# Hierarchical MoE step: expert rows weighted as they leave PSUM, and accumulated by DMA into the outputs

## What is computed

```python
def hierarchical_moe(h, ...):                     # h = rmsnorm(x1), t = its 320 rows
    g_prob = softmax(t @ w_router_group + b);  g_p, g_idx = top_k(g_prob, 1)
    e_prob = softmax(logits of the 8 experts of that group);  e_p, e_idx = top_k(e_prob, 2)
    e_p = e_p / sum(e_p);      combine = one_hot(e_idx) * e_p * g_p, by group
    for g in range(N_GROUPS):                     # dense in the reference
        hg = silu(t @ w_gate[e]) * (t @ w_up[e])
        out = out + (hg * combine[e]) @ w_down[e]
return x1 + out
```

## Time and profile before

| | us |
|---|---|
| median of three executions | 906.62 |
| the profiled execution, its own time | 908.45 |
| its span on the core | 907.0 |

### The profile page before, as it was taken

The page is one execution under the profiler, slowest core; times in us unless marked ns, Lnnn a source line. Parts: engine busy times, 40 slices in busy tenths (PEclk is TensorE's granted clock), DMA queues, the critical chain, the costliest instruction groups (busy, mean ns, idle before and its releaser), DMA issues.

```text
span 907.0 us, 14392 instructions
## 1 busy us (share of the span) xinstructions
PE 763.5 (84%) x5476; PEld 605.1 (67%) x5476; DVE 401.9 (44%) x936; ACT 300.8 (33%) x552; POOL 144.4 (16%) x245
## 2 busy tenths in 40 slices
PE   2999999977799898999778898989399999787780
PEld 1788999965456588999666678988274555444440
DVE  3574334454345443657455545773753222111113
ACT  5434354533323343556222224443421111111110
POOL 5001000002134200011231310000302222222210
PEclk9999999987789989999998989999699999999996
DMA  5233433223568615273575551893849999999985
GB/s 177 95 139 132 142 139 134 94 78 132 151 190 243 207 41 186 94 250 132 191 247 158 169 183 54 333 352 142 327 167 418 417 418 418 420 419 419 417 335 184
DMA packets 38170, 202.84 MB, mean 224 GB/s; under 512 B 7490, under 2 KB 8018, under 8 KB 18898
## 3 DMA queue, kind: packets, MB, share of 16 engines
q1 hardware_dynamic: 24434, 160.29, 46.0%
q0 software_dynamic: 13664, 41.58, 14.4%
HBM read 184.24 MB, written 23.38 MB: 229 GB/s over the span
## 4 chain that ended last, share of the span: by engine, by line
PE 54%; DMA 17%; DVE 13%; ACT 8%; issue 6%; POOL 0%; POOLq 0%; SPq 0%; DVEq 0%; ACTq 0%
PE bank L1677 18%; DMA fm<-in_w_moe 9%; PE bank L1681 7%; PE bank L2020 6%; DVE rm L1089 3%; PE bank L1832 3%; DMA em<-in_w_moe 3%; ACT rm L773 3%; PE bank L2040 3%; PE bank L1667 3%; PE bank L1881 2%; PE bank L1916 2%; PE bank L2001 1%; DMA fm<-in_cache_lf 1%; PE bank L1821 1%
## 5 line engine op out<-in xcount | busy, mean ns | idle before, releaser
L1677 PE MATMUL bank<-rm 128*128 128x320 f32 x1344 | 211.4, 317 | 2.4 <-issue 1.6
L1677 PEld LDWEIGHTS bank<-rm 128*128 128x128 f32 x1344 | 202.7, 193 | 7.7 <-issue 6.1
L1089 DVE TENSOR_TENSOR rm<-fm,rm 128x2048 fp32r<-128x2048 f32 x48 | 110.1, 2293 | 83.5 <-ACT rm L773 83.0
L1681 PE MATMUL bank<-rm 128*128 128x256 f32 x960 | 126.5, 292 | 7.2 <-DVE rm L1089 3.6
L1681 PEld LDWEIGHTS bank<-rm 128*128 128x128 f32 x960 | 122.1, 199 | 8.4 <-DVE rm L1089 3.8
L773 ACT ACTIVATE rm<-fm 128x2048 fp32r<-128x2048 f32 x48 | 91.9, 1915 | 25.7 <-PE bank L1677 16.9
L2022 PE MATMUL bank<-fm,em 128*64 128x256 f32 x384 | 96.6, 397 | 0.0
L2020 PE MATMUL bank<-em 128*64 128x256 f32 x272 | 68.1, 395 | 9.6 <-DMA fm<-in_w_moe 4.8
L2020 PE MATMUL bank<-fm,em 128*64 128x256 f32 x240 | 60.3, 397 | 12.6 <-DMA fm<-in_w_moe 11.3
L2020 PEld LDWEIGHTS bank<-em 128*64 128x64 f32 x272 | 36.2, 141 | 36.8 <-issue 22.1
L1052 ACT ACTIVATE fm<-bank 64x256 f32<-64x256 f32 x32 | 12.0, 376 | 136.5 <-PE bank L2022 136.5
(11 more groups left out here) (388 smaller groups left out, 1032.8 us busy)
## 6 DMA issues: line engine op xcount, KB each, us to landing
fm<-in_w_moe SPq DMA_DIRECT2D x57, 1024.0 KB, 26.6
fm<-in_w_dense SPq DMA_DIRECT2D x48, 1024.0 KB, 4.9
em<-in_w_moe SPq DMA_DIRECT2D x39, 1024.0 KB, 26.1
fm<-in_state_C POOLq DMA_DIRECT2D x32, 257.0 KB, 4.2
out_C_sample<-fm POOLq DMA_DIRECT2D x32, 257.0 KB, 5.3
fm<-in_cache_kT POOLq DMA_DIRECT2D x16, 512.0 KB, 5.0
fm<-in_cache_v POOLq DMA_DIRECT2D x16, 512.0 KB, 4.5
fm<-y_rows SPq DMA_DIRECT2D x4, 512.0 KB, 5.1
```

The lines of the kernel that those rows point to most:

```text
L1089: s(TT(pair[c % 2][1], cube(raw[c % RAW1], KC), pair[c % 2][0], ALU.subtract), sem("split_done"))
L1677: ins = mm(bank[b][:, 0:NT], w[:, k, P * u:P * (u + 1)], a[:, k, :], start=first, stop=final)
L1681: ins = mm(bank[b][0:r, 0:CW], a[:, k, TILE0[u]:TILE0[u] + r], w[:, k, :], start=first, stop=final)
```

## The change

Outputs take the place of `y_rows`. SP, not POOL, stores x1 three times: to `y_prompt`, to `y_sample` and to `x1_dram`, ahead of weight load 14; both waits for `x1_stored` now ask for all three. `hot` is widened to `hot_rw` (row number, and weight), and the matmuls for the row numbers become twelve of 64 columns instead of six of 32; they move ahead of `start(0)`. `w_slot` is each place's weight, and `take_y` multiplies by it: ACT by `scale`, DVE by a `tensor_scalar`. The DVE steps for ranks, weights and `at_rank` move in between the copies of the sort.

The experts run in another order: `expert(v)` takes one of each group in turn. So v and v + 1 (v even) are of different groups and share no token. POOL no longer scatters after each expert, but after each second one, both halves of `y_area` (128 rows) at once, as two indirect DMAs that add to what is there: one on `y_prompt`, one on `y_sample`. `take_y(v)` for v >= 2 waits for both DMAs of the pair before: 32 times the number of earlier pairs. The end goes: no reload of x1, no read-back, no combining, no output stores outside `crowd`.

```diff
-        y_rows = nc.dram_tensor("y_rows", [6 * P, D], F32).ap()
+        y_rows = O["y_prompt"].rearrange("p t d -> (p t) d")
...
+        def expert(v):
+
+            return v % NG * EPG + v // NG
...
-                sp.dma_start(slot[n % NSLOT], A["w_moe"][3 * v + j]).then_inc(landed(v, j)[0], 16)
+                sp.dma_start(slot[n % NSLOT], A["w_moe"][3 * expert(v) + j]).then_inc(landed(v, j)[0], 16)
...
                 elif n == 14:
+                    sp.wait_ge(sem("x1_full"), 1)
+                    sp.dma_start(O["y_prompt"], x1[:, 0:2, :]).then_inc(sem("x1_stored"), 16)
+                    sp.dma_start(O["y_sample"], x1[0:NS, 2, :]).then_inc(sem("x1_stored"), 16)
+                    sp.dma_start(x1_dram, x1).then_inc(sem("x1_stored"), 16)
...
-            pool.wait_ge(sem("x1_full"), 1)
-            pool.dma_start(x1_dram, x1).then_inc(sem("x1_stored"), 16)
...
                     pool.wait_ge(sem("e_y_left"), v + 1)
                     pool.wait_ge(sem("e_y_right"), v + 1)
-                    pool.indirect_dma_start(y_rows, bass.IndirectOffsetOnAxis(ap=row_i[:, v:v + 1].bitcast(U32), axis=0),
-                                            yrow[v % NY], None, bounds_check=6 * P - 1, oob_is_err=False)\
-                        .then_inc(sem(f"e_y_stored{v % NY}"), 16)
+                    if v % 2 == 0:
+                        continue
+                    for rows, place, n in ((y_rows, row_i, TP), (O["y_sample"], row_s, NS)):
+                        idx = place[:, expert(v - 1):expert(v - 1) + 1].bitcast(U32)
+                        pool.indirect_dma_start(rows, bass.IndirectOffsetOnAxis(ap=idx, axis=0), y_area, None,
+                                                bounds_check=n - 1, oob_is_err=False, compute_op=ALU.add)\
+                            .then_inc(sem("e_y_stored0"), 16)
...
                 act.wait_ge(sem("e_used"), unit(v, 2) + 1)
+                if v == 0:
+                    act.wait_ge(sem("rows_ready"), 1)
                 if v >= NY:
-                    act.wait_ge(sem(f"e_y_stored{v % NY}"), 16 * (v // NY))
-                A_(yrow[v % NY][:, 0:D // 2], bank[4 + v % 2][0:CAP, :], ACT.Copy).then_inc(sem("e_y_left"), 1)
+                    act.wait_ge(sem("e_y_stored0"), 32 * (v // NY))
+                A_(yrow[v % NY][:, 0:D // 2], bank[4 + v % 2][0:CAP, :], ACT.Copy,
+                   scale=w_slot[0:CAP, expert(v):expert(v) + 1]).then_inc(sem("e_y_left"), 1)
...
                 dve.wait_ge(sem("e_used"), unit(v, 2) + 1)
                 if v >= NY:
-                    dve.wait_ge(sem(f"e_y_stored{v % NY}"), 16 * (v // NY))
-                CP(yrow[v % NY][:, D // 2:D], bank[4 + v % 2][CAP:2 * CAP, :]).then_inc(sem("e_y_right"), 1)
+                    dve.wait_ge(sem("e_y_stored0"), 32 * (v // NY))
+                TSC(yrow[v % NY][:, D // 2:D], bank[4 + v % 2][CAP:2 * CAP, :], w_slot[CAP:2 * CAP, expert(v):expert(v) + 1],
+                    None, ALU.mult).then_inc(sem("e_y_right"), 1)
...
-            dve.wait_ge(sem("xe_in"), 16 * 3)
-            s(CP(wts[NS:P, 2, :], wts[0:NS, 2, :]))
-            for t in range(3):
-                n = D if t < 2 else D // 2
-                dve.wait_ge(sem(f"rows_of_y{t}"), 32 if t < 2 else 64)
-                for k in range(2):
-                    s(STT(xe[:, t, 0:n], gat[2 * t + k][:, 0:n], wts[:, t, k:k + 1], xe[:, t, 0:n], ALU.mult, ALU.add),
-                      sem("y_done") if k else None)
...
-            start(0)
             pe.wait_ge(sem("onehot"), 3 + 6)
             for k in range(2):
                 for t in range(3):
                     i, r = 3 * k + t, ROWS[t]
-                    ins = mm(bank[6][0:CAP, 0:NE], at_rank[i][0:r, :], hot[k][0:r, t, :], start=(i == 0), stop=(i == 5))
+                    for half in range(2):
+                        ins = mm(bank[6][CAP * half:CAP * (half + 1), 0:2 * NE], at_rank[i][0:r, :], hot_rw[k][0:r, t, :],
+                                 start=(i == 0), stop=(i == 5), skip_group_check=True)
             ins.then_inc(sem("router_full"), 1)
+            start(0)
```

The DVE part of the sort, shortened:

```diff
+            for n in range(1, 2 * KC, 2):
+                k, half = n // 2, n % 2
+                dve.wait_ge(sem("sorted_full"), n + 1)
+                s(CP(xs[:, k, NT * half:NT * (half + 1)], bank[n % 4][:, 0:NT]), sem("sorted_free_v"))
+                if k < 2:
+                    ranks(k)
+                elif k == 2:
+                    combine()
+                elif k < 5:
+                    hot_rows(k - 3)
+                elif k < 7:
+                    at_ranks(k - 5)
```

More of the change, by code:

```diff
@@ L317, in hybrid_step @@
         offs = take(NE)
+        hot_rw = [cube(take(3 * 2 * NE), 3) for _ in range(2)]
         assert top[0] <= FW
+        w_slot, not_sample = (fm[:, base_masks + 1296 + NE * i:base_masks + 1296 + NE * (i + 1)] for i in range(2))
         squares, lgT = em[:, 12288 + 384:12288 + 384 + CW], em[:, 12288 + 640:13312]
@@ L498, in _ @@
                 load(n)
[L500 to L503, removed]
             def crowd():
+                sp.wait_ge(sem("blocks_stored"), 1)
+                sp.dma_start(xe[:, 0:2, :], x1_dram[:, 0:2, :]).then_inc(sem("xe_in"), 16)
+                for rows, w in SIDES:
+                    sp.dma_start(xe[rows, 2, 0:D // 2], x1_dram[0:NS, 2, w]).then_inc(sem("xe_in"), 16)
                 sp.wait_ge(sem("xe_in"), 16 * 3)
@@ L514, in crowd @@
                                 .then_inc(c_in, 16)
-            for u in range(NY):
-                sp.wait_ge(sem(f"e_y_stored{u}"), (NE - u + NY - 1) // NY * 16)
-            for t in range(2):
-                for k in range(2):
[L520 to L525, removed]
-            either(sp, crowd, sp.nop)
-            for t in range(3):
[L529 to L535, removed]
+                for t in range(3):
+                    sp.wait_ge(sem("y_done"), t + 1)
+                    if t < 2:
+                        sp.dma_start(O["y_prompt"][:, t, :], xe[:, t, :]).then_inc(sem("y_out"), 16)
+                    else:
+                        for rows, w in SIDES:
+                            sp.dma_start(O["y_sample"][:, w], xe[rows, t, 0:D // 2]).then_inc(sem("y_out"), 16)
+                sp.wait_ge(sem("y_out"), 16 * 4)
+            either(sp, crowd, sp.nop)
         @block.gpsimd
@@ L700, in run_experts @@
                 pool.wait_ge(sem("rows_ready"), 1)
+                pool.wait_ge(sem("x1_stored"), 16 * 3)
                 for v in range(NE):
@@ L1539, in _, with ranks @@
             s(v.tensor_reduce(most[:, 0:1], bank[4][:, 0:NE], AX_X, ALU.max))
[L1540 to L1549, removed]
+            def ranks(k):
                 s(TT(esel, hot[k], offs.unsqueeze(1).broadcast_to([P, 3, NE]), ALU.mult))
@@ L1552, in _, with combine @@
                 s(TT(scal[3 * k], place[:, :, k], scal[3 * k + 1], ALU.subtract))
[L1553 to L1560, removed]
+            def combine():
                 dve.wait_ge(sem("router_exps"), 1)
@@ L1567, in late_words, with hot_rows, at_ranks @@
                 s(TT(wts[:, :, 1], wts[:, :, 0], second, ALU.mult))
+            def hot_rows(k):
+                s(TT(hot_rw[k][:, :, 0:NE], hot[k], row_of.unsqueeze(2).broadcast_to([P, 3, NE]), ALU.mult))
+                s(TT(hot_rw[k][:, :, NE:2 * NE], hot[k], wts[:, :, k:k + 1].broadcast_to([P, 3, NE]), ALU.mult))
+            def at_ranks(k):
+                for t in range(3):
+                    s(TSC(at_rank[3 * k + t][0:ROWS[t], :], iota[0:ROWS[t], 0:CAP], scal[3 * k][0:ROWS[t], t:t + 1], None,
+                          ALU.is_equal), sem("onehot"))
+            dve.wait_ge(sem("x1_stored"), 16 * 3)
+            s(v.memset(xs[:, :, SLOTS:XC], 0.0))
+            for n in range(1, 2 * KC, 2):
[10 more added lines that the diff above has]
+                    at_ranks(k - 5)
+            dve.wait_ge(sem("sorted_free_a"), KC)
+            s(v.memset(small[0:1, 94:95], 0.0), sem("xs_ready"))
+            dve.wait_ge(sem("router_full"), 6)
+            s(TSC(not_sample, bank[6][:, 0:NE], float(TP - NO_ROW), float(NO_ROW), ALU.is_lt, ALU.mult))
+            for part, w, o in ((slice(0, CAP), slice(0, NE), slice(0, NE)),
+                               (slice(CAP, 2 * CAP), slice(EPG, NE), slice(0, NE - EPG))):
+                s(TSC(row_i[part, o], bank[6][part, w], float(NO_ROW), None, ALU.add))
+                s(STT(row_s[part, o], bank[6][part, w], float(NO_ROW - TP), not_sample[part, w], ALU.add, ALU.add))
+            s(CP(w_slot, bank[6][:, NE:2 * NE]), sem("rows_ready"))
+            def late_words():
                 crowd3 = crowd_i.rearrange("p (t k) -> p t k", t=3)
@@ L1612, in crowd @@
                 dve.wait_ge(sem("c_free"), NE * JB + 1 + 4)
[L1614 to L1623 removed]
+                s(CP(wts[NS:P, 2, :], wts[0:NS, 2, :]))
+                for t in range(3):
+                    n = D if t < 2 else D // 2
+                    for k in range(2):
```

(3 more changed lines are left out.)

32 lines of the change are left out of this document (16 added, 16 removed).

## The result

The changed kernel takes 938.5 us in the median (934.5 to 943.1) against 907.5 for the kernel before on the same chip: a ratio of 1.036, interval 1.031 to 1.041. It is slower, by 3.6%. The forecast was slower by 1.7%. The profiled execution of after took 935.45 us.

What follows compares the result with a forecast made beforehand. PE sets the pace first, the weight stream later, then a tail without weights. First pair at 690.6, twelve pairs of 16.2 us to 885.0, plus 32.9 and 5, make 922.9; less 0.4, rounded to 922 us, range 894 to 948.

Steps and rivals of the forecast that it cites:

- the chain behind the wait: From a pair's landing through take_y, htp copy, down matmuls and copy to POOL's next issue: 4.7 us.
- the tail: After the last copy, from the last pair's first issue to the kernel's end: 5 us, bounds 3.5 and 9.
- The wait itself: take_y of the next expert waits until both DMAs of the pair before land; a pair takes 16.2 us.
- Start of the experts: Row-number matmuls add 1.2 to 2 us, moved DVE steps save 1.1; first pair issued at 690.6, within 1 us.
- The store of x1: Moved to SP's queue ahead of load 14, landed at about 652 before DVE's wait at 660.31: cost 0.
- L: From a pair's first issue to its second DMA's landing, under the weight stream: 11.5 us, later 5 us.
- the formula: Landing time: 4.1 us lead, 0.31 us per packet for a load packet plus its own time, 0.5 to land.
- the third rival: Accumulates cost two turns or wait on memory, 958 us; or PE's clock is lower in gaps, 950 us; chance 0.10.
- slots that never hold the loads: Weight stream: 21 slots hold seven experts and six are left after pair 12, so slots don't hold the loads.
- The last three pairs: After the weights end: two pairs at PE's 11.2 us and a last one of 8.9, 32.9 us with the clock.
- The tail that goes: Landing, read-back, combining and stores after the last issue, 20.4 us before, shrink to 5: gain 15.4 us.

Runs made afterwards that it cites:

- e2: Changed kernel plus six useless matmuls on PE ahead of each second expert's downs, v = 3 to 29: 1.040 of the kernel before.
- e4: Changed kernel with plain writes instead of additions in the pair's DMAs: 1.019 of the kernel before, 922.6 us.
- e6: Changed kernel with a second y_area in place of one weight slot and the closing wait on SP: 0.988 of the kernel before, 895.5 us.
- e9: e6 without the addition, so that the DMAs overwrite: 0.982 of the kernel before, 890.9 us.
- e5: Changed kernel with the closing wait for the accumulating DMAs on SP instead of POOL: 1.030 of the kernel before, 936.5 us.
- e8: Changed kernel plus six useless matmuls on PE ahead of odd experts' downs only up to v = 25: 1.031 of the kernel before, 934.4 us.

## Why the prediction was right in sign and short in size

The step that failed is the chain behind the wait: it was put at 4.7 us and measured 6.2, since the gap that the wait makes lets PE's clock fall and the down matmuls take 2.8 to 3.7 us instead of 1.9 (e2 gives the 4.7 back). A second term, the tail, was put at 5 us and measured 9.6. The wait itself, its place and its landing were right.

The span was forecast at 922.9 and is 934.0. The 11.1 us are four terms: -7.0 at the start, +10.6 in twelve pairs, +2.9 in the last three, +4.6 after the last issue.

- **Start of the experts** (forecast 690.6, measured 683.65). The moved edits cost nothing, as forecast: from the issue of the x1 store to the first pair it took 54.0 us before and 53.7 after (630.00 to 683.65). The 7 us come from ahead of the change. PE ran for 44 us at its lower clock before 620 us, against 68 in before, and over the ten kernels profiled with the change the first pair's issue lay between 683.0 and 692.3, on the whole later the more such time there was (44 to 72 us). Why one execution has more of it than another isn't settled. It also means that the forecast, put on a start like before's, would have missed by 18 us, not 11: that the miss is no larger is luck.
- **The store of x1**: three stores, issued at 630.0 to 631.1, landed when DVE passed its wait at 654.19 with 0.17 us idle. Its cover held.
- **L** (forecast 11.5; measured 11.4 to 12.0 in eight of the ten long pairs, 12.4 and 13.0 in two, mean 11.85). The term that the case hung on was right. Its parts were 4.8 us of lead, not 4.1, and 0.33 us a data packet, as assumed. With the 4.8 the formula gives 12.2, so it is good to some 0.4 us and no better. The Trainium skill (DMA: Bandwidth & Descriptors, section "Anatomy of one DMA"), with about 2.0 us plus bytes at 436 GB/s, would have it near 5 by the prediction's estimate: the runs show 11.4 to 13.0 us beside a full load queue and 5.6 to 6.1 once the weights are in. For the landing that a wait sees, the rule was of use here only with the queue of the loads empty.
- **The chain** (forecast 4.7, measured 5.7 to 6.5, mean 6.2): the step that failed. Its down matmuls were priced at the 1.9 us of a stretch without gaps, though the forecast itself makes the gap of 4 to 5 us before each of them. The lower clock was named, in the third rival, as a possible load on PE's slack, with 17.5 us a pair; it belonged in the forecast's own chain. The rival's 950 puts 17.5 on all sixteen pairs, though the last three have no weights beside them: in the forecast's own sum it gives 690.6 + 12 x 17.5 + 32.9 + 5 = 938.5. Measured, 11.85 + 6.2 make the 18.0 us that ten of twelve pairs took, 1.8 over the forecast: 1.5 by the chain and 0.35 by L. `take_y` with its factor took 0.76, not 0.69; copy to issue 1.61, not 1.53.
- **Gaps in the weight stream.** The forecast had slots that never hold the loads. In two pairs SP waited for slots and the load queue was short all the same, and they got off with 12.3 us, 3.9 under the forecast each. So ten pairs at +1.8 and two at -3.9 make the +10.6; without the two gaps, which the forecast did not have, the miss would have been larger. PE never waited for weights, as forecast: no weight load stands among what released it. The weights ended at 885.5, also as forecast.
- **The last three pairs** (forecast 32.9, measured 35.8). The forecast took the last one at PE's pace, 8.9 us; it is the chain again and took 12.6: 6.1 us to the release, 6.5 with the slow downs. The two before took 11.56 by POOL's longer issues; with plain writes (e4) they took 11.18.
- **The tail** (forecast 5, measured 9.6): 5.6 to landing, then POOL's DRAIN. The view that would have shown it is the list of the closing instructions, in which before has its 5.2 us hidden.
- **The tail that goes** was worth what was said, seen without the wait: in e6 7.6 us follow the last issue instead of 20.4, and 12.8 are gained. 2.1 of them are lost again, as the last issue is at 888.73 instead of 886.62; without the added reads (e9) it is at 882.54. That leaves the 10.7 us between the spans 907.0 and 896.3. These are single executions, whose first pairs were issued 8.2 us apart (691.29 and 683.05); the medians are 8.7 us apart (904.2 and 895.5).

## What to carry to other kernels

When a transfer takes over work, ask who waits for its landing, and price that landing beside the traffic that will run there: here it was 18 packets an engine, each behind a packet of a load, and rows that carry nothing took such a turn like rows that do. Price the chain that follows at the clock that its own new gaps will bring. A second buffer paid for by one of 21 weight slots turned 3.6% slower into 1.2% faster, with the closing wait moved.

## What was not expected of the hardware

- An accumulating indirect DMA of 128 rows takes POOL 1.57 us to issue, a plain one 0.97; its data packets hold an engine for 0.327 us, plain ones 0.160.
- POOL's closing DRAIN took 3.18 us in after and 5.22 in before, in both with all of POOL's DMAs landed. In e5, started while they were in flight, it took 5.48 and ended 1.6 us after the landing.
- With gaps of 4.1 to 5.5 us ahead of eight matmuls, these ran at the lower clock level for part or all of their time in each of the ten long pairs (2.8 to 3.7 us instead of 1.9); with matmuls of no use in the gap (e2, e8) they took 1.9 in every pair.
